# High and low halves of four matmul operands at other distances, modulo 256 bytes, to the weight ring

## The reference

```python
z = rmsnorm(x, g) @ w_in                 # in_a, in_b, in_sb, in_fox: queries, keys, values
x = x + attention(z) @ w_out             # out_a ... out_fox
x = x + relu(rmsnorm(x, g) @ w_up)**2 @ w_down          # up_a, down_a, up_b, down_b
x = x + rmsnorm((gelu(conv(gate)) * conv(up)) @ w_down)  # up_sb, down_sb, up_fox, down_fox
```

## The kernel before

| buffer | before | after |
|---|---|---|
| h1_hi, h1_lo | 192, 192 | 192, 128 |
| h2_hi, h2_lo | 192, 64 | 64, 192 |
| a_hi, a_lo | 192, 192 | 64, 64 |
| o_hi, o_lo | 192, 192 | 128, 192 |
| H, ZM, mv_tok, wf_hi, wf_lo | 64 | 192 |
| ident, ones, rope tables, masks | 128 | 0 |
| square, rstd, sumsq, log_ms | 64 | 192 |
| Z, ROT, conv_buf, prod | 192 | 64 |
| v_tok, s_buf, n_buf, c_buf, p_buf, pt_buf, fcum | 192 | 192 |

## Time and profile before

### The profile page before, as it was taken

How to read it: one execution, slowest core, us unless ns; L and a number is a source line. 1 busy time by engine, 2 the same in 40 slices (tenths; PEclk the granted TensorE clock), 3 DMA queues, 4 the chain that set the end, 5 groups by cost and what they waited for, 6 DMA issues and landing times. The chain is left out here.

```text
span 1342.6 us, 29554 instructions
## 1 busy us (share of the span) xinstructions
PE 1258.1 (94%) x9952; PEld 1189.0 (89%) x9952; DVE 949.3 (71%) x1545; ACT 732.5 (55%) x1307; POOL 478.1 (36%) x465
## 2 busy tenths in 40 slices
PE   7988999999997999999998789999999999999996
PEld 7977999999985999999896589998988978999896
DVE  6599667655588676644679568998466766899844
ACT  6556554444454554434546456666455555666642
POOL 2231255300022255300212248887020004888711
PEclk8999899999998999999999699999999999999998
DMA  7544365555643455655543134555754333455472
GB/s 272 173 142 126 117 198 187 173 187 187 189 150 102 132 190 184 189 184 187 165 133 124 51 111 164 177 172 142 201 174 157 127 102 118 156 176 172 144 205 85
DMA packets 63287, 212.40 MB, mean 158 GB/s; under 512 B 7793, under 2 KB 8945, under 8 KB 62833
## 3 DMA queue, kind: packets, MB, share of 16 engines
q1 hardware_dynamic: 63216, 211.50, 49.4%
HBM read 207.28 MB, written 1.05 MB: 155 GB/s over the span
## 5 line engine op out<-in xcount | busy, mean ns | idle before, releaser
L1129 DVE TENSOR_TENSOR w_lo<-raw,w_hi 128x1024 fp32r<-128x1024 f32 (+2 forms) x408 | 508.6, 1253 | 143.6 <-ACT w_hi L816 143.6
L816 ACT CAST w_hi<-raw 128x1024 fp32r<-128x1024 f32 (+2 forms) x408 | 407.7, 1004 | 268.3 <-PE bank L500 186.4
L498 PE MATMUL bank<-h_hi,w_hi 128*128 128x256 f32 x1168 | 332.3, 285 | 6.6 <-DVE w_lo L1129 4.0
L499 PE MATMUL bank<-h_lo,w_hi 128*128 128x256 f32 x1168 | 329.3, 282 | 0.0
L500 PE MATMUL bank<-h_hi,w_lo 128*128 128x256 f32 x1168 | 327.6, 281 | 0.0
L1498 POOL TENSOR_TENSOR sumsq<-sumsq,square 128x256 f32<-128x256 f32 x107 | 95.6, 893 | 474.3 <-ACT square L828 291.0
L498 PE MATMUL bank<-a_hi,w_hi 128*128 128x256 f32 x896 | 253.5, 283 | 10.9 <-DVE w_lo L1129 9.5
L499 PE MATMUL bank<-a_lo,w_hi 128*128 128x256 f32 x896 | 252.7, 282 | 0.0
L500 PE MATMUL bank<-a_hi,w_lo 128*128 128x256 f32 x896 | 252.7, 282 | 0.0
L498 PEld LDWEIGHTS bank<-h_hi,w_hi 128*128 128x128 f32 x1168 | 220.0, 188 | 13.9 <-issue 12.9
L500 PEld LDWEIGHTS bank<-h_hi,w_lo 128*128 128x128 f32 x1168 | 221.4, 190 | 0.0
(11 more groups left out here) (154 smaller groups left out, 2111.4 us busy)
## 6 DMA issues: line engine op xcount, KB each, us to landing
raw<-in_w_up_sb SPq DMA_DIRECT2D x44, 512.0 KB, 3.3
raw<-in_w_up_fox SPq DMA_DIRECT2D x44, 512.0 KB, 3.3
raw<-in_w_up_a SPq DMA_DIRECT2D x32, 512.0 KB, 3.4
raw<-in_w_down_a SPq DMA_DIRECT2D x32, 512.0 KB, 4.5
raw<-in_w_up_b SPq DMA_DIRECT2D x32, 512.0 KB, 3.4
raw<-in_w_down_b SPq DMA_DIRECT2D x32, 512.0 KB, 4.4
raw<-in_w_in_sb SPq DMA_DIRECT2D x24, 512.0 KB, 4.0
raw<-in_w_in_fox SPq DMA_DIRECT2D x24, 512.0 KB, 4.3
```

The source lines that it names most:

```text
L498: nc.tensor.matmul(dst, w_hi[:, slot, w], src_hi[:, at + k, :], start=begin, stop=False)
L499: nc.tensor.matmul(dst, w_hi[:, slot, w], src_lo[:, at + k, :], start=False, stop=False)
L816: nc.scalar.copy(w_hi[:, slot, 0:k * P], raw[:, slot, 0:k * P]).then_inc(hi_ready, 1)
L1129: nc.vector.tensor_tensor(w_lo[:, slot, 0:k * P], raw[:, slot, 0:k * P], w_hi[:, slot, 0:k * P].bitcast(f32), ALU.subtract).then_inc(lo_re ...
```

## The change

Four unused buffers are put between the operands; every instruction, wait and transfer stays as it is.

```diff
         X = sb("X", [P, KT, TOK])
         sb("lead_h1", [P, 48])
         h1_hi = sb("h1_hi", [P, KT, TOK], f32r)
+        sb("lead_h1_lo", [P, 48])
         h1_lo = sb("h1_lo", [P, KT, TOK], f32r)
+        sb("lead_h2", [P, 48])
         h2_hi = sb("h2_hi", [P, KT, TOK], f32r)
         sb("lead_h2_lo", [P, 32])
         h2_lo = sb("h2_lo", [P, KT, TOK], f32r)
...
         ROT = sb("ROT", [P, 4, TOK])
+        sb("lead_o", [P, 16])
         o_hi = sb("o_hi", [P, KT, TOK], f32r)
+        sb("lead_o_lo", [P, 16])
         o_lo = sb("o_lo", [P, KT, TOK], f32r)
```

## The result

The changed kernel takes 1354.2 us in the median of 12 runs (1351.0 to 1358.8) beside 1346.3 us for the kernel before on the same chip (1343.1 to 1350.6). The ratio is 1.006, 95% interval 1.0044 to 1.0075: slower by 0.6%, about 8 us. The forecast was 5.3 us faster; the time lies inside the stated range, and the difference is near rival 3's +8. The lines of the changed kernel are 4 higher: 498 to 500 became 502 to 504, 468 to 470 became 472 to 474.

What follows compares the result with a forecast made beforehand. PE, busy for 94% of 1342.6 us, was taken as the main bound, shared with DVE or POOL in some stages; -9.1 + 2.3 + 1.5 = -5.3 us took 1349.8 to 1344.5 us, range 1331 to 1358.

Steps and rivals of the forecast that it cites:

- rival 3: All gemm operands: 64, 64 no better for a, o and h1 lose the quick pace; +8 us, 1357.8 us; chance 0.27.
- The bound by stage, two paces with the same instructions, a start that draws and a stream that keeps: PE bounds some stages, shares others; triples take 340 or 353 ns, a pattern taken at a start and kept until interrupted.
- a, -9.1 us: Down projections, a from 192, 192 to 64, 64: 680 slow triples turn quick, -9.1 us; other end +2.2.
- o, +2.3 us: Output projections, o from 192, 192 to 128, 192: three stages lose the quick pace, +2.3 us; other end -0.8.
- h1, +1.5 us: in_ stages, h1 from 192, 192 to 192, 128: 220 quick triples turn slow, half counted, +1.5 us; ends -1.4 and +2.9.
- h2, 0: Up projections, h2 from 192, 64 to 64, 192: stays slow, 0 us; ends -6.7 and +1.8.
- values, 0: The values stages, where the ring streams past h1: h1_lo's distance comes to 128; 0 us, 1.7 us either sign.
- DVE, ACT and POOL, 0: Their buffers move as well; 0 us, with bounds of 2 us either way from a 1% change in DVE's 949 us.
- Sum: Whole kernel: the terms of a, o and h1 together, -9.1 + 2.3 + 1.5 = -5.3 us.

Runs made afterwards that it cites:

- gap_down: One extra matmul of constants ahead of down_a and of down_b, distances as in the kernel before; single time 1343.6 us beside a median of 1344.7.
- h2_equal: Against the kernel before, only h2_lo goes from 64 to 192, so all four operands are at 192, 192; ratio 0.992, 1332.9 us beside 1344.2.
- a_only: Against the kernel before, only a (with conv_buf and prod) goes from 192, 192 to 64, 64; slower by 0.28%.
- equal_64: All four operands put at 64, 64 against the kernel before; ratio 1.0058.
- h1_only: Against the kernel before, only h1_lo goes from 192 to 128, so h1 is at 192, 128; slower by 0.23%.
- o_only: Against the kernel before, only o_hi goes from 192 to 128, so o is at 128, 192; slower by 0.27%.
- ring_shift: An unused buffer of 64 bytes ahead of raw moves the ring and all else together, distances as in the kernel before; ratio 0.9989.
- map_1: Against the kernel before, equal halves with h1 at 160, h2 at 224, a at 32, o at 96; single time 1356.4 us beside 1342.5.
- map_2: Against the kernel before, equal halves with h1 at 32, h2 at 96, a at 224, o at 160; single time 1360.4 us beside 1342.5.

## Why the prediction was wrong

- **The bound by stage, two paces with the same instructions, a start that draws and a stream that keeps**: right. gap_down and h2_equal show what the earlier trace rows only suggested. Two readings on the way were off without harm: down_sb's stage has a granted clock of 0.97 and not 1.00 (its low stretch ends ahead of the row's 941.8), and the values' 336 ns is an effect of rounded starts; from start to start the trace has 340. That PE's extra time in up_sb and up_fox is covered: right, as up_sb keeps its length at either pace.
- **a, -9.1 us**: this step failed. It took the nearest rows to be those of the values, where the ring is the moving and h1 the stationary operand, and carried their quick pace over to a gemm at 64, 64. In a_only and equal_64 every down projection, at 64, 64, runs at 353 ns. The term measured 0 in down_a, down_b and down_fox and +2.0 us of pace in down_sb: the other end that the prediction gave (+2.2). The likeness of a difference modulo 256 between two streams with exchanged roles and lengths was no likeness of the case. The rows of a itself, slow in all or most of three of four stages at the old distances, were nearer.
- **o, +2.3 us**: right in its sign and too small; +1.9, +0.3, +1.3 and +2.4 make +5.9, of which by the granted clocks some 1.7 is clock and 4.2 pace. The prediction had two paces to choose from, and the distances 128, 192 brought a third, 363 ns, in three of four stages. It bounded the loss by the slow pace, where wf's 357 had already shown that a triple can take longer than 353.
- **h1, +1.5 us**: right in its sign; +1.6 in in_a and +2.1 in the other three make +3.7, above its upper end of 2.9. Two sizes were off. The pace that 192, 128 brings is 356 to 357 ns (h1_only), not 353; and the half that DVE was to hide was not hidden in in_a, which grows by 1.6 us at a granted clock of 1.00 both times, more than the price of some 72 lost triples (72 x 13.3 ns = 1.0, or 1.2 at the pace measured).
- **h2, 0**: right. up_a and up_b are 0.4 to 0.5 us shorter, at the same pace.
- **values, 0**: mis-sized, +0.9, within the 1.7 that it was bounded by. The values were quick with h1 at 192, 192, and are not with h1 at 192, 128.
- **DVE, ACT and POOL, 0**: right; DVE's busy time went from 949.3 to 950.2 us.
- **Sum**: with the measured terms a +1.9 (2.0 of pace, -0.1 of clock), o +5.9, h1 +3.7, h2 -0.9 it is +10.6, and with the values +11.5, of the 12.4 us by which the two spans differ. Rival 3 had the mechanism (a no better at 64, 64, o and h1 out of the quick pace, a slower pace for distances of 128) and +8 us; the medians differ by 7.9. That the two figures meet is in part luck, as its slow pace for o was 357 and not 363, and the profiled spans differ by 12.4.
- **The page "SBUF — State Buffer" of the Trainium skill**, section "Who interferes with whom", would have given 0 by "PE and ACT never wait on anyone". The runs decide against what the prediction drew from it, that addresses change nothing: down_a takes 360.0, 353.3, 356.1 and 340 ns a triple with all four operands at 0, 64, 128 and 192, with no other difference than unused buffers. Whether the two reads wait for one another is not shown.

Two things stay open. Why the paces are what they are: the runs give a table, not a mechanism, and the form "the moving and the loading stream meet in SBUF" is argued, not shown. And what makes a start draw one pace or the other at 192, 192. With a's distances untouched, down_fox stays quick from its first to its last triple in h1_only and o_only, and turns slow in before, gap_down and ring_shift, though h1_only has a gap like that of the earlier trace rows at the same place (0.37 us between two starts):

```profile
L501 PE MATMUL bank<-a_lo,w_hi x176: 276/276/283, 1270.4 to 1332.7; 128*128 128x256 f32 x176
```

So the layout does not fix the draw; as no kernel was traced twice, these runs can't say what does. The spread of single runs (5 to 12 us in the kernels with ten or more) may come from this, but no run here tests it.

## What to carry to other kernels

When a stream of weight loads and matmuls bounds a stage, read the time from start to start of one line, not the shown duration: the distance modulo 256 bytes between the moving operand and the weights can be worth 6% of it, and both parts of a split operand count. Of the eight equal distances and four unequal pairs here, 192 for both was the only one at which long streams ran at 340 ns, so in a kernel with these shapes it is the first to try: moving one unused buffer of 128 bytes from ahead of h2_lo to behind it gained 0.8%. It is no guarantee, as a stream at 192 can also run at 353. Price a layout that no row shows from the same operand in the same role, and where starts draw between two paces, look at several stages before calling one of them the layout's.

## What the hardware showed that was not expected

Time of one triple (three matmuls of 256 columns with their weight loads of 128) at full granted clock, by the distance of both halves to the weights:

| distance, bytes | 0 | 32 | 64 | 96 | 128 | 160 | 192 | 224 |
|---|---|---|---|---|---|---|---|---|
| ns | 360 | 350 or 353 | 353, rarely 340 | 360 | 356 or 360 | 356 or 352 | 340 or 353 | 355 |

Unequal halves: 192, 64 and 64, 192 gave 353; 128, 192 gave 353, 360 or 363; 192, 128 gave 356 to 357. So a choice between two paces is not peculiar to 192; what sets 192 apart is that long streams have 340. The order of the distances is neither monotonic nor periodic in 64. The distances 32, 96, 160 and 224 rest on one execution each of map_1 and map_2. A stage at 192, 192 can change between 340 and 353 at an interruption of a third of a microsecond, and a single foreign matmul at a stage's start was enough to turn 353 into 340 for the 87 us behind it, both times that it was tried. Other distances of DVE's, ACT's and POOL's operands, in the changed kernel, left their busy times within 1.3 us of where they were.

At 363 ns the time between two starts of line 503 alternates: in out_a of the changed kernel they stand at 150.06, 150.43 and 150.79 us, 0.37 and 0.36 apart. So this pattern is longer than a triple.
